# A fused decoder block on one Trainium2 core: GLA's first queries and keys run before the shift is known, and the first modulation's pieces are divided anew between TensorE and VectorE

## The reference

```python
mod = silu(c) @ w_ada + b_ada            # shift1, scale1, gate1, shift2, scale2, gate2
h = rms_norm(x, g_norm1) * (1.0 + scale1) + shift1
proj = h @ w_in        # gq gk gv gg ga_low | fq fk fv f_logit | gate_a gate_b
o_a = gated linear attention(gq, gk, gv, decay from ga_low), normed, times silu(gg)
o_b = forgetting attention(fq, fk, fv, f_logit), 16 heads of 128
merged = sigmoid(gate_a) * (o_a @ w_proj_gla) + sigmoid(gate_b) * (o_b @ w_proj_fox)
x = x + gate1 * (merged @ w_out)
x = x + gate2 * (square(relu(h2 @ w_ff1)) @ w_ff2)     # h2 like h, with shift2, scale2
return rms_norm(x, g_final)
```

## Time and profile before

| | |
|---|---|
| time, 3 runs | 1877.29 us median (1874.05 to 1877.8) |
| profiled execution | 1874.23 us, its span 1872.5 us |
| PE busy | 1829.5 us, 98% of the span |
| DVE busy | 1232.6 us, 66% |
| ACT busy | 847.8 us, 45% |
| DMA | 441.50 MB, mean 236 GB/s |
| mean granted TensorE clock | 0.991 |

### The profile page before, as it was taken

One profiled execution on the slowest core, in us unless ns is written; L12 is line 12 of the kernel. 1 busy time (PEld: TensorE's weight loads), 2 busy tenths in 40 slices (PEclk: granted clock), 3 DMA queues, 4 the chain that ended last, 5 costly groups with the idle time before them and its releaser, 6 DMA issues.

```text
span 1872.5 us, 21674 instructions
## 1 busy us (share of the span) xinstructions
PE 1829.5 (98%) x8351; PEld 1485.3 (79%) x8351; DVE 1232.6 (66%) x1367; ACT 847.8 (45%) x1075; POOL 21.3 (1%) x44
## 2 busy tenths in 40 slices
PE   6998999999999999999999998999999999999998
PEld 3666888888888888888888886888888888888886
DVE  5997667676666667666666777775555555555555
ACT  4444555455544444344344444443444344434443
POOL 1000000000000000000000000000000000000000
PEclk8999999999999999999999998999999999999999
DMA  9998898899987987999899784886666666666663
GB/s 383 401 319 250 215 225 282 244 239 250 210 212 243 216 236 245 252 255 301 265 263 265 255 281 163 280 277 197 194 184 182 197 191 187 187 196 189 185 191 124
DMA packets 214767, 441.50 MB, mean 236 GB/s; under 512 B 18437, under 2 KB 34917, under 8 KB 214282
## 3 DMA queue, kind: packets, MB, share of 16 engines
q1 hardware_dynamic: 213272, 436.57, 78.2%
q10 hardware_dynamic: 1138, 3.50, 0.5%
q0 software_dynamic: 256, 0.05, 0.0%
HBM read 437.92 MB, written 2.10 MB: 235 GB/s over the span
## 4 chain that ended last, share of the span: by engine, by line
PE 89%; DVE 2%; issue 1%; DMA 1%; ACT 1%; SPq 0%; POOL 0%; ACTq 0%; POOLq 0%; DVEq 0%
PE ps L1749 82%; PE ps L1733 1%; PE ps L1853 1%; DVE wlo L1172 0%; PE ps L1905 0%; DMA raw<-in_w_in 0%; PE ps L1657 0%; PE ps L1659 0%; DVE xT L1575 0%; PE ps L1862 0%; ACT whi L711 0%; DVE obT L1579 0%; DMA raw<-in_w_ff 0%; PE ps L1788 0%; PE ps L1801 0%
## 5 line engine op out<-in xcount | busy, mean ns | idle before, releaser
L1172 DVE TENSOR_TENSOR wlo<-raw,whi 128x1024 fp32r<-128x1024 f32 x604 | 738.5, 1224 | 580.1 <-ACT whi L711 578.7
L711 ACT ACTIVATE whi<-raw 128x1024 fp32r<-128x1024 f32 x604 | 639.3, 1059 | 928.3 <-PE ps L1749 713.7
L1749 PE MATMUL ps<-whi,hT 128*128 128x512 f32 x2304 | 742.8, 397 | 4.8 <-DVE wlo L1172 4.5
L1749 PEld LDWEIGHTS ps<-whi,hT 128*128 128x128 f32 x2304 | 435.1, 189 | 113.6 <-DVE wlo L1172 12.5
L1749 PE MATMUL ps<-wlo,hT 128*128 128x512 f32 x1152 | 450.6, 391 | 0.0
L1749 PE MATMUL ps<-whi,obT 128*128 128x512 f32 x1280 | 403.8, 393 | 3.8 <-DVE wlo L1172 2.6
L1749 PE MATMUL ps<-whi,oaT 128*128 128x512 f32 x1248 | 389.0, 390 | 0.0
L1749 PEld LDWEIGHTS ps<-whi,obT 128*128 128x128 f32 x1280 | 242.0, 189 | 56.1 <-DVE wlo L1172 4.0
L1749 PEld LDWEIGHTS ps<-whi,oaT 128*128 128x128 f32 x1248 | 234.3, 188 | 49.0 <-issue 0.5
L1749 PEld LDWEIGHTS ps<-wlo,hT 128*128 128x128 f32 x1152 | 217.7, 189 | 45.4 <-issue 2.2
L1749 PE MATMUL ps<-wlo,obT 128*128 128x512 f32 x640 | 250.4, 391 | 0.0
(11 more groups left out here) (236 smaller groups left out, 786.8 us busy)
## 6 DMA issues: line engine op xcount, KB each, us to landing
raw<-in_w_ff SPq DMA_DIRECT2D x256, 512.0 KB, 3.9
raw<-in_w_in SPq DMA_DIRECT2D x248, 512.0 KB, 6.9
raw<-in_w_ada SPq DMA_DIRECT2D x128, 512.0 KB, 5.4
first<-in_w_ada SPq DMA_DIRECT2D x64, 512.0 KB, 9.9
raw<-in_w_in SPq DMA_DIRECT2D x64, 256.0 KB, 6.7
raw<-in_w_proj_fox SPq DMA_DIRECT2D x32, 512.0 KB, 5.7
raw<-in_w_proj_gla SPq DMA_DIRECT2D x32, 512.0 KB, 5.8
raw<-in_w_out SPq DMA_DIRECT2D x32, 512.0 KB, 5.0
```

Of the source, the lines that this page charges most:

```text
L711: nc.scalar.activation(parts(g)[0][:], raw[POS_G[g] % RING][:], ACT.Copy).then_inc(s_hi, 1)
L1172: V.tensor_tensor(rest[:], raw[POS_G[g] % RING][:], top[:].bitcast(F32), ALU.subtract).then_inc(s_lo, 1)
L1749: i = T.matmul(ps[bank(name, t)][:], src[:, kt, hl, tk], w[:, k, :], start=(kt == 0 and n == 0), stop=(kt == KT - 1 and n == 2))
```

## The change

Three things change.

- All 8 units of qk0 also run on h without the shift. Units 0 to 31 (`READY`) run in the first stage, and the shifted h is first used by unit 32. 8 more "w" rides and an `acck` accumulate what shift1 adds to gq0 and gk0; a fourth `shift_sum` and `shift_add` put it in.
- The pieces are divided anew. PE takes whole pieces: 7 in group 0 (k = 2, 4, ..., 14), 6 in group 1 (k = 1, 4, 6, 9, 11, 13), none in groups 2 and 3. It uses the piece itself as eight 128 x 128 weights with `cond[k]` as the one moving column, accumulating in the PSUM columns that `sum_first` also adds to. DVE takes the other 51 pieces whole. The bias `b_ada` enters through four small loads (`brow`) and two small matmuls at the start; `bih`, the row and its additions are gone.
- The hand-written order follows: new `LOAD_AT`, `SPLIT` and `RUN`; in groups 2 and 3 PE runs units up to 21 before the third sum and up to 32 before the fourth; the small loads of the gate columns move from position 28 of the stream to 36; the rides are spread anew.

```diff
+def on_pe(p):
     n, k = PIECE[p]
-    return p > P_LAST[n] - 2 or (k % 4 != 1 if n else k in (0, 7))
+    return k in ((2, 4, 6, 8, 10, 12, 14), (1, 4, 6, 9, 11, 13), (), ())[n]
...
-LOAD_AT = [13, 14, 15] + [17 + 7 * _i // 4 for _i in range(9)] + [32] + [33 + 2 * _i for _i in range(1, 12)] + [57, 59, 61]
-FOX_EARLY = 2
+EARLY = 8
+READY = G_FOX + EARLY
+LOAD_AT = [14, 15, 16, 17, 19, 20, 22, 23, 25, 26, 28, 29] + [31 + (142 * _i + 50) // 100 for _i in range(READY + LEAD - 12)]
+def later(p, lead):
+    return max(0, -(-(2295 * (p - 31) - lead) // 3440))
+for _p in range(PIECES):
+    LOADED[_p] = sum(_a <= _p for _a in LOAD_AT)
+    if P_0[1] <= _p < P_0[2]:
+        RUN[_p] = (1, 1, 1, 3, 3, 3, 4, 4, 4, 6, 6, 7, 7, 8, 8, 9)[_p - P_0[1]]
+        SPLIT[_p] = (4, 4, 4, 5, 5, 6, 6, 7, 8, 8, 9, 9, 10, 10, 12, 12)[_p - P_0[1]]
+    elif _p >= P_0[2]:
+        RUN[_p] = max(13, 12 + later(_p, 11600)) if on_pe(_p) else 21 if _p < P_0[3] else READY
+        SPLIT[_p] = max(14, 13 + later(_p, 4100))
...
-SHIFTS = KT + UG
-SHIFT_Q = (25, 27, 30, 32, 35, 37, 40, 42)
-SHIFT_AT = {46: 0}
+SHIFTS = UG + KT + UG
+SHIFT_Q = (33, 34, 36, 37, 39, 41, 43, 44)
+SHIFT_AT = {47: 0}
...
-        g += 5 if g < 43 else 2 if g < G_GLA else 3 if g < G_MIX or n % 2 else 2
+        g += 2 if g < G_GLA or g >= G_MIX else 3
...
             def ada_first(p):
                 n, k = PIECE[p]
...
-                T.matmul(ps[6][0:1, :], cond[:, k:k + 1], first[p % FRING][:, 0:NB],
-                         start=(p == p0), stop=(p == p1)).then_inc(s_adp, 1)
+                for j in range(8):
+                    c = n // 2 * 8 + j
+                    i = T.matmul(ps[6 + n % 2][:, c:c + 1], first[p % FRING][:, j * P:j * P + P], cond[:, k:k + 1],
+                                 start=False, stop=False, skip_group_check=True)
+                i.then_inc(s_adp, 1)
...
             run = 0
             for p in range(PIECES):
-                ada_first(p)
+                if on_pe(p) or p in P_LAST:
+                    while run < RUN[p]:
+                        if run == READY - 1:
+                            turn(("fq", 0), fqk_tok)
+                        row_unit(run)
+                        run += 1
+                if on_pe(p):
+                    ada_first(p)
                 if p in P_LAST:
-                    sum_first(P_LAST.index(p))
+                    sum_first(PIECE[p][0])
...
+            for p in range(P_0[1]):
+                if not on_pe(p):
+                    ada_first(p)
...
+            lo(0)
+            split = norm1_chunk(0, 1)
...
+            for p in range(P_0[1], PIECES):
+                if p == P_0[2] + 1:
                     split = norm1_chunk(1, split)
-                if p == P_0[3]:
+                if p == P_0[3] + 5:
                     mod_first(2)
...
+                if not on_pe(p):
+                    if p != P_0[2]:
+                        split = split_to(split, SPLIT[p])
+                    ada_first(p)
```

More of the change, by code:

```diff
@@ L571, in load @@
                                  ).then_inc(s_raw[pos % RING], 16)
-                elif kind == "w" and what >= UG:
+                elif kind == "w" and UG <= what < UG + KT:
                     both = w_in_v[:, what - UG, C_GV:C_GV + 2 * (C_GG - C_GV)].rearrange("p (a n) -> p a n", a=2)
@@ L910, in _ @@
                     hi(12 + kt // 4 - 2)
-            for g in range(14, 27):
+            for g in range(14, READY + LEAD):
                 hi(g)
@@ L925, in _ @@
                 if kt == 11:
-                    hi(G_FOX + LEAD)
+                    hi(READY + LEAD)
             for it in range(4):
-                for u in range(24):
-                    if it or u:
+                for u in range(0 if it else EARLY, 24):
+                    if it or u > EARLY:
                         hi(G_FOX + 24 * it + u + LEAD)
-                    if it == 0 and u == 5:
-                        stage(("fq", 0), fqk_tok)
-                    if it == 0 and u == 0:
+                    if it == 0 and u == EARLY:
                         act.dma_start(wup[0:RANK, :, :], w_gla_a_up[0].rearrange("r (a n) -> r a n", n=NB)
@@ L1131, in ada_first @@
                 dve.wait_ge(s_fraw[p % FRING], 16 * (p // FRING + 1))
-                if p == P_0[n]:
-                    dve.wait_ge(s_bih, n * 16 + 16)
+                if not any(P_0[n] <= m and not on_pe(m) for m in range(p)):
                     if n > 1:
                         dve.wait_ge(s_modmm, 2 * n - 2)
[L1136 to L1145, removed]
+                    V.tensor_scalar(b, a[:], cond[:, k:k + 1], None, ALU.mult).then_inc(s_ada, 2)
+                    return
+                dve.wait_ge(s_ada, 2 * pieces_dve(p - 1))
+                V.scalar_tensor_tensor(b, a[:], cond[:, k:k + 1], b, ALU.mult, ALU.add).then_inc(s_ada, 2)
             def mod_first(n):
@@ L1226, in shift_piece @@
                     rows = [(accq[:], r[:, k, :], KU * j + k, 1) for k in range(KU)]
+                elif j >= UG + KT:
+                    rows = [(acck[:], r[:, k, :], KU * (j - UG - KT) + k, 1) for k in range(KU)]
                 else:
@@ L1760, in _ @@
             T.transpose(ps[3][:, 0:2 * KT], vrow[:], ident[0:2 * KT, 0:2 * KT]).then_inc(s_vt, 1)
+            pe.wait_ge(s_brow, 64)
+            for b in range(2):
+                T.matmul(ps[6 + b][:, 0:KT], brow[:], ident[0:2 * KT, b * KT:b * KT + KT], start=True, stop=False,
+                         skip_group_check=True)
             pe.wait_ge(s_cond, 1)
@@ L1778, in _ @@
                     norm_turn(p - 6)
-                while run < RUN[p]:
-                    row_unit(run)
-                    run += 1
             def small_cols():
@@ L1951, in _ @@
                             decay_sums()
-                    if it == 0 and u == 7:
-                        turn(("fq", 0), fqk_tok)
                     if u == 10:
```

159 lines of the change are left out of this document (80 added, 79 removed).

## The result

The changed kernel takes 1895.89 us (median of 4 runs, 1894.87 to 1896.76), the kernel before 1875.85 us on the same chip (4 runs, 1874.05 to 1877.8): ratio 1.0106, 95% interval 1.0089 to 1.0124. It is 1.1% slower. The profiled execution took 1895.92 us, its span 1894.2, which is 21.7 us more than that of before. The forecast was +3.1 between profiled executions, so 18.6 us are to be explained. (The forecast of 1880.4 added another 3.1 us for the median over the profiled execution; with the fourth run of before the medians lie 1.6 us above it before and at it after, 20.0 us apart.)

A forecast was written before the change was run, and what follows sets the result against it. PE is busy throughout from about 165 us, so unit 32's start decides: +2.1 us there and +1.0 for the added sum on 1874.2 give 1877.3. Another 3.1 for the median gives 1880.4 us, range 1864 to 1887.

The forecast's parts named there:

- the likeliest sign: For the whole kernel's time, the forecast gave slower 0.42, same 0.33 and faster 0.25.
- the chain of groups 2 and 3: PE and VectorE up to the fourth sum: unit 32 starts effectively at 166.0 us, against 163.9 before, +2.1.
- Group 0: Seven whole pieces on PE at the low clock, 3.50 us each, put the first sum's end at 47.6 us.
- Rival A: PE keeps pace with arrivals in group 0, first sum ends 14 us earlier, total 1866.4 us; chance 0.22.
- Group 1: From the first unit at 49.4 us, nine units, six pieces at 1.76 and a sum end at 88.7.
- rival B: The low clock returns after each of group 1's six pieces, adding 10 us, total 1890; chance 0.10.
- Group 2: VectorE is done at 124.6 us; PE waits 3 us, sums until 126.5, then runs low for a while.
- Cost as above 1.7: Behind the third sum, a low-clock stretch on PE costs 1.7 us.
- Group 3: VectorE's 35.4 us and about 2.3 of waiting end piece 63 at 162.3; unit 32 partly low, 1.8.
- Removed after it: PE's waits at 147 to 160 us go; this is already counted in the 163.9 us for unit 32.
- Added after it: After unit 32, one shift_sum costs 0.9 to 1.0 us on PE; the 8 added rides cost nothing.
- rival C: The added rides reach PE in units 192 to 319, up to 10 us, taken at half, 1885; chance 0.08.

The follow-up runs named there:

- g0_dve: The changed kernel with VectorE taking all 16 of group 0's pieces and PE none: 1888.68 us, 1.0055 of the kernel before.
- run23: The changed kernel with PE running 23 units instead of 21 before the third sum: 1897.52 us, 1.0105 of the kernel before.
- the two stage runs: The kernel before with fq0 staged at the third unit rather than the sixth: 1874.84 us; with the small loads also at position 34 instead of 28: 1875.97 us.
- qk_rows: The changed kernel with qk0's units loaded as rows of 2 KB instead of 1 KB (keys' columns not the reference's): 1888.83 us, 1.0063 of the kernel before.
- three_causes: The changed kernel with group 0's pieces all on VectorE, the seventh modulation half summed two units later, and qk0 in 2 KB rows: 1877.03 us, 0.9999.
- no_qk_rides: The changed kernel without the 8 added rides, the fourth shift_sum and its additions: 1891.05 us, 1.0074 of the kernel before.
- before_qk_rows: The kernel before with units 24 to 31 loaded as rows of 2 KB (keys' columns not the reference's): 1872.63 us, 0.9976 of the kernel before.
- late_mod: The changed kernel with the seventh modulation half's two sums at units 360 and 362 instead of 358 and 360: 1891.6 us, 1.0077 of the kernel before.

## Why the prediction failed where it did

**The dates of the first three sums held to within 1.1 us; the loss that I missed came behind them.** Slower was the likeliest sign, and 3.1 us of it were worked out where 21.7 were measured. Three steps failed: the chain of groups 2 and 3, 6.4 us too short; the stretch from unit 32 to the scores, for which the sum had no term, 3.9 us; and "I take nothing" for what the added rides do, 8.3 us.

*Group 0: confirmed.* Forecast: low clock throughout, 3.50 us a piece, 0.9 a turn, first sum ending at 47.6, first unit at 49.4. Shown: 3.28, 0.87 (24.65 - 22.91 for two), 46.5 and 47.68. g0_dve shows that it costs, and how much: 0.5%. Of the 8.9 us at the first sum 6.4 are left at the fourth. Rival A, that PE keeps pace, is out. A load and its matmul together had a period of 205 ns at the low clock (3.28 us for 16) and of 106 at the high one (1.70 for 16). *TensorE: Matmul & The Clock Gate*, section LDWEIGHTS, in the Trainium skill gives a load as its columns over 1.2 ns, 107 ns for 128, and names no clock level. The high level agrees with that; the low one does not, and there the measured period stands. The durations of the loads in groups 0 and 1 differ in the same way (source view of L1739, ns least/median/most):

```profile
L1739 PEld LDWEIGHTS ps<-cond,first x112: 285/333/337, 12.7 to 42.7; 128*128 128x128 f32 x112
...
L1739 PEld LDWEIGHTS ps<-cond,first x96: 187/192/192, 52.1 to 82.2; 128*128 128x128 f32 x96
```

*Group 1: confirmed.* Second sum ending at 88.7 forecast, 87.8 shown. All six pieces took 1.84 us, so rival B, a low stretch after each, is out.

*Group 2: confirmed, then mis-sized.* VectorE done at 124.6 forecast; the sum began at 124.28 after 3.72 us of waiting (forecast 3). "Cost as above 1.7" was wrong: I took one short stretch of low clock, and it was 10.2 us long (123.3 to 133.6). In the change that delayed unit 21 and with it VectorE by 4.56 us where I had 2.3.

*Group 3: the step that failed in the first stage.* "Piece 63 is done at 162.3" was 167.1. Of the 4.8 us, 2.3 are that longer wait, and 2.7 are four waits of VectorE, for pieces or their issue, which I left out. Group 3 had no term for late arrivals: I had set the stream at 401 GB/s throughout, and it moved 286 from 124 to 152 us. The timeline of VectorE after (L1176 splits, L1149 pieces):

```profile
134.37 1.22 DVE L1176 TENSOR_TENSOR wlo<-raw,whi 128x1024 fp32r<-128x1024 f32 x1 [4.56 <-ACT whi L720]
...
143.66 1.29 DVE L1149 SCALAR_TENSOR_TENSOR acch<-first,cond,acch 128x1024 f32<-128x1024 f32 x1 [0.58 <-DMA first<-in_w_ada]
...
147.80 1.28 DVE L1149 SCALAR_TENSOR_TENSOR acch<-first,cond,acch 128x1024 f32<-128x1024 f32 x1 [0.93 <-issue]
...
153.13 1.28 DVE L1149 SCALAR_TENSOR_TENSOR acch<-first,cond,acch 128x1024 f32<-128x1024 f32 x1 [0.92 <-DMA first<-in_w_ada]
...
156.61 1.28 DVE L1149 SCALAR_TENSOR_TENSOR acch<-first,cond,acch 128x1024 f32<-128x1024 f32 x1 [0.27 <-issue]
...
165.82 1.28 DVE L1149 SCALAR_TENSOR_TENSOR acch<-first,cond,acch 128x1024 f32<-128x1024 f32 x1
```

The last of these lines is piece 63. The two aren't separate costs: run23 removed the first and the fourth sum stayed. The sum then ran at the low clock (2.94 instead of 1.9 to the next start) and unit 32 lost 2.4 instead of 1.8. Together 6.4 us.

*"Removed after it": right in the main.* The turn of fq0 waited 0.85 us instead of 3.19. But its place was taken, as the two stage runs show for the kernel before.

*Unit 32 to the scores: no step at all.* I let everything after unit 32 move by one amount. The low clock came in at the decay logits: 0.9 us on them, 2.3 on the next three units, and 0.8 more of an issue wait, 3.9 in all. In the profiled executions it is absent in before, qk_rows, three_causes and no_qk_rides, and a stretch of 3.4 or 6.8 us begins under the decay logits or within 0.3 us of their end in the ten others, before_qk_rows and the two stage runs among them. What starts it is not settled. The date alone does not: the decay logits begin at 179.40 in three_causes, without it, and at 179.51 in before_qk_rows, with it. So it is not shown that this step belongs to the change.

*"Added after it ... I take nothing": the largest single miss, 8.3 us.* I asked whether the DMAs or VectorE would be full in units 192 to 319. They nearly were not: PE waited 1.2 us for splits and 0.5 for a turn's data there, so rival C's mechanism is there and its price is not. I didn't ask whether the modulation halves, which share the rides' places, would still be complete when PE sums them. late_mod shows that one was not, at 0.3%. In before_qk_rows, where that last piece is still at unit 354, the same sum waits 1.06 us, so there was no slack to begin with. Of the rest, 2.8 us before the second norm, 1.7 are those four small waits, which no run isolates.

Three of the prediction's figures are slightly off and change nothing: two pieces arrive every 2.61 us and not 2.56, 265 x 188/176 is 283, and VectorE's terms of group 3 add up to 35.2.

**What stays open:** about 4.3 us between three_causes and before_qk_rows, of which 1.0 is by estimate the added `shift_sum`; whether the change makes the short rows dearer; and the low clock at the decay logits.

## What to carry to other kernels

Work given to an idle engine at its slow level can cost more than leaving the engine idle: compare its price at that level (here 3.28 us a piece) with what the other engine takes (1.2) and with the arrivals (1.31), and try the engine idle. When helpers that share slots (here rides) grow in number, recompute the completion date of every consumer behind them, not only the load of the engines. And before crediting the removal of a wait, look for what starves the waiting engine: if the stream is late, the wait moves one instruction down.

## What the runs showed of the hardware

Full weight loads with one-column matmuls, and eight turns among them, kept PE busy from 12.68 to 46.5 us without raising its clock: 3.28 us for the 16 pairs of a piece, against 1.70 behind dense units. Giving PE nothing for 8.10 us there (g0_dve) was better. The clock column of the windows doesn't show this: for 12 to 22 us of the change it has

```profile
12.00:22.00 10.00, 9.32 (x44) 9.35 (x45) 6.57 (x10) 2.65 (x3) 0.71 (x1) 1.00 1.03 409
```

where the loads' 333 ns are those of the low level. Rows of 1 KB instead of 2 KB lowered the DMA's rate from 380 to 286 GB/s at the same busy share, in windows of 28 us in which pieces with rows of 4 KB land as well. The packets of 1 KB took 46 ns in the median, but 87 on average. *DMA: Bandwidth & Descriptors*, section Why small descriptors are slow (HBM only), in the Trainium skill gives a fixed overhead of about 3 cycles a packet beside one cycle for 32 bytes. An estimate from that page is 67 cycles for a row of 2 KB and 70 for two of 1 KB, 4% apart; the two runs differ by 25%, and that stands. And the eight matmuls of the decay logits, over 17 rows, took 3.69 us in before and 4.59 in the change, whose clock fell to 0.50 under them at 195.0 us, though PE had been busy without a gap since 178 us and runs the same units around them.
